# Moving GpSimd's steps of a woven-in chain two gathers later, and one accumulation three rows later

## The reference

```python
u_sel = jnp.take(u, idx, axis=0)
act = jax.nn.gelu(jnp.einsum("chkd,cd->chk", u_sel, xc))
v_sel = jnp.take(v, idx, axis=0)
return jnp.einsum("chk,chkd->cd", act * gates, v_sel)
```

## Time and profile before

| what | value |
| --- | --- |
| median of 3 runs | 2394.14 us (2394.11 to 2395.13) |
| the profiled execution's own time | 2392.49 us |
| its span | 2390.5 us |
| TensorE, VectorE, ScalarE, GpSimd busy | 85%, 74%, 49%, 30% of the span |
| mean rate of the transfers | 325 GB/s over the span |

### The profile page before, as it was taken

How to read it: one execution, slowest core, us unless ns; L and a number is a source line. 1 busy time by engine, 2 the same in 40 slices (tenths; PEclk the granted TensorE clock), 3 DMA queues, 4 the chain that set the end, 5 groups by cost and what they waited for, 6 DMA issues and landing times. The chain is left out here.

```text
span 2390.5 us, 29684 instructions
## 1 busy us (share of the span) xinstructions
PE 2041.0 (85%) x9896; PEld 1414.8 (59%) x9896; DVE 1768.2 (74%) x3454; ACT 1174.1 (49%) x3850; POOL 728.1 (30%) x637
## 2 busy tenths in 40 slices
PE   8899897687875568999666687799989999999999
PEld 8544442243331127874343565588459978898997
DVE  6589876766778878889899988766765646756564
ACT  4355566665565563433455554433344435444443
POOL 0134434453444443233365633433310001100000
PEclk9999998998986688999885798899989999999999
DMA  9199999999999998999999999999976544224553
GB/s 361 72 398 421 415 384 351 398 395 404 398 415 387 395 396 344 400 421 420 362 405 356 376 421 420 399 417 421 421 295 208 177 166 146 89 89 159 194 178 139
DMA packets 109767, 777.72 MB, mean 325 GB/s; under 512 B 12320, under 2 KB 13088, under 8 KB 16688
## 3 DMA queue, kind: packets, MB, share of 16 engines
q0 software_dynamic: 73728, 536.90, 55.6%
q1 hardware_dynamic: 35888, 238.93, 26.0%
HBM read 773.69 MB, written 2.10 MB: 325 GB/s over the span
## 5 line engine op out<-in xcount | busy, mean ns | idle before, releaser
L2102 ACT ACTIVATE smalls<-smalls 128x1 f32<-128x1 f32 (+1 forms) x2058 | 541.3, 287 | 716.8 <-DVE smalls L2006 698.9
L2830 POOL DMA_INDIRECT pair<-in_uv,idx x512 | 609.5, 1190 | 913.5 <-DVE resid L1265 495.8
L663 PE MATMUL bank<-pair,diag 128*64 128x512 f32 (+1 forms) x1056 | 314.2, 710 | 142.5 <-ACT diag L2102 142.2
L2006 DVE CUSTOM_DVE_ANT_0 pair<-pair,hd 128x1024 f32<-128x1024 f32 x256 | 311.7, 1221 | 148.2 <-DMA pair<-in_uv,idx 147.2
L663 PE MATMUL bank<-ft,raw 128*128 128x256 f32 x1664 | 371.1, 385 | 17.9 <-DVE ft L1259 17.9
L663 PEld LDWEIGHTS bank<-ft,raw 128*128 128x128 f32 x1664 | 321.3, 194 | 63.4 <-issue 18.4
L2006 DVE CUSTOM_DVE_ANT_0 pair<-pair,hn 128x1024 f32<-128x1024 f32 x256 | 312.2, 1220 | 56.9 <-DMA pair<-in_uv,idx 56.4
L1265 DVE SCALAR_TENSOR_TENSOR resid<-pair,smalls,resid 128x1024 f32<-128x1024 f32 x243 | 310.8, 1279 | 0.7 <-ACT smalls L2102 0.6
L1259 DVE TENSOR_TENSOR half<-raw,half 128x1024 fp32r<-128x1024 f32 (+2 forms) x184 | 212.0, 1191 | 122.7 <-ACT half L2102 121.2
L663 PEld LDWEIGHTS bank<-pair,diag 128*64 128x64 f32 (+1 forms) x1056 | 77.2, 155 | 319.3 <-ACT diag L2102 191.4
L2102 ACT ACTIVATE half<-raw 128x1024 fp32r<-128x1024 f32 (+2 forms) x184 | 179.5, 1023 | 90.9 <-PE bank L663 90.8
(11 more groups left out here) (328 smaller groups left out, 3183.1 us busy)
## 6 DMA issues: line engine op xcount, KB each, us to landing
raw<-in_wts SPq DMA_DIRECT2D x199, 1024.0 KB, 8.9
pair<-in_wts SPq DMA_DIRECT2D x11, 1024.0 KB, 16.8
pair<-in_uv,idx POOLq DMA_INDIRECT x512, 10.7
raw<-in_wts SPq DMA_DIRECT2D x10, 512.0 KB, 6.2
raw<-in_wts SPq DMA_DIRECT2D x4, 720.0 KB, 6.1
resid<-in_x SPq DMA_DIRECT2D x4, 512.0 KB, 12.0
out<-resid SPq DMA_DIRECT2D x8, 256.0 KB, 5.7
raw<-in_wts SPq DMA_DIRECT2D x2, 768.0 KB, 6.5
```

The lines of the kernel that those rows point to most:

```text
L663: return e.matmul(o, a, b, start=start, stop=stop)
L2006: e.tensor_tensor_reduce(b[:, 0:1024], b[:, 0:1024], x_, 1.0, 0.0, ALU.mult, ALU.add, actv[:, i % 8:i % 8 + 1]).then_inc(dotted, 1)
L2102: return e.activation(o, i, f, **kw)
L2830: e.indirect_dma_start(pair[i % NPAIR], None, uv, bass.IndirectOffsetOnAxis(ap=idx[:, n % SLOTS, k:k + 1], axis=0)).then_inc(pairs_in[i % ...
```

## The change

Two numbers are changed. GpSimd does the steps of chain A two gathers later in its order: a step that stood ahead of gather i stands ahead of gather i + 2. And VectorE adds the banks of the third tile (`mixed_in(2, ...)`) in its row 271 instead of 268. No instruction is added or taken away.

```diff
                     for strand in strands:
                         strand.until(i)
-                    if i == HALF + 12:
+                    if i == HALF + 15:
                         mixed_in(2, i - 1)
                         for h in range(2):
                             taken(e, "mix", 4 + h)
...
             first, between = Paced(chain("A")), Paced(rest())
             for i in range(PAIRS):
                 n, k = divmod(i, 16)
-                first.until(clock(i - 8))
+                first.until(clock(i - 10))
                 between.until(i)
```

## The result

The changed kernel takes 2405.14 us (median of 7 runs, 2399.74 to 2410.42), the kernel before 2393.32 us (7 runs, 2386.42 to 2395.13). The ratio is 1.0061, 95% interval 1.0046 to 1.0075: 14.6 us more, between 11 and 18 (the two medians lie 11.8 us apart). The prediction was 2408.0 us, range 2397 to 2414, "slower" at 0.81. Its forecast case came true. Run again later, beside the kernel before on the same chip, the changed kernel gave 1.0058 (1.0037 to 1.0080).

The account below looks back on a forecast made before the run. TensorE and the DMA transfers were taken to be at their limit together. Terms -1.3 + 0 + 2.8 + 6.7 + 1.0 + 4.7 sum to +13.9 us, giving a median of 2408 us, range 2397 to 2414.

Parts of the forecast that it names:

- forecast case: Whole kernel: the likeliest outcome, +10 to +19 us, 2404 to 2413 us, chance 0.55.
- mixed_in: Moved from row 268 to 271, it lets TensorE's first up-projection start earlier: -1.3 us, bounds 0 and -1.3.
- first norm's rates: Run after gather 271 instead of before 270; VectorE has no wait: 0 us, upper bound +1.
- second norm: Rates behind gather 336 make VectorE and the latent projection wait: +2.8 us, bounds 0 and +3.8.
- latent and head rates: VectorE 9.5 us late at row 351, less 2.8 of gather waits: +6.7 us, bounds +3 and +9.5.
- attention's head rates: Pairs used at rows 366 and 384; gather waits cover VectorE's delay, gathers land later: +1 us, bounds -2 and +5.
- third norm: Rates behind gather 448 make VectorE wait, and all reaches the end: +4.7 us, bounds +2.3 and +5.3.
- row rule: GpSimd steps due at row d run once VectorE added row d+4, not d+2; uses four rows after due stall.
- its own 5 us are covered there: Attention, 1378 to 1450 us: VectorE's 13.4 us of gather waits cover its own 5 us delay.
- Rival 1: Norms and head rates: the queue of transfers hides much of the stalls, +5.4 us, 2399.5 us, chance 0.22.
- Rival 2: GpSimd's steps: none of their move reaches the end, only mixed_in is left, 2393 us; chance 0.11 including mixtures.
- Rival 3: Transfer holes, above all at 1270 us, go as gathers aren't held behind steps: faster, 2385 us, chance 0.07.

Follow-up runs that it names:

- again: The changed kernel's second run and profile, both edits unchanged, against the kernel before on the same chip: 2405.66 against 2391.08 us, ratio 1.0058.
- i - 6: All of GpSimd's steps two gathers earlier than in the kernel before, mixed_in left in row 268: ratio 0.9971 (0.9960 to 0.9982).
- i - 7: All of GpSimd's steps one gather earlier than in the kernel before, mixed_in left in row 268: ratio 0.9992 (0.9979 to 1.0004).
- mixed_in alone: Only mixed_in moved to row 271, GpSimd's order that of the kernel before: ratio 0.9998 (0.9983 to 1.0014).
- i - 9: All of GpSimd's steps one gather later than in the kernel before, mixed_in left in row 268: ratio 1.0015 (1.0003 to 1.0027).
- latent and head rates alone: Only the three latent rates and four head rates of fq and fk two gathers later than in the kernel before: ratio 1.0031 (1.0017 to 1.0045).

## Why the prediction was right, term by term

| term | predicted | measured by rows |
| --- | --- | --- |
| mixed_in | -1.3 (0 to -1.3) | -0.5, -1.3 again, -1.6 alone, at row 273 |
| first norm's rates | 0 | 0, no wait at L1259 |
| second norm | +2.8 (0 to 3.8) | +2.9 in four profiles |
| latent and head rates | +6.7 (3 to 9.5) | +7.8 - 1.6 = +6.2 |
| attention's head rates | +1.0 (-2 to +5) | +6.1 - 2.7 = +3.4 |
| third norm | +4.7 (2.3 to 5.3) | +5.1 to +6.2 |
| sum | +13.9 | +17.6 by rows 267 to 511; +14.6 by the runs' ratio |

The total came out nearer than its terms, and that is in part luck. By rows the loss is 3.7 us more than forecast: attention was 2.4 us dearer, mixed_in gave 0.8 less, and 0.9 lie in rows 333 to 343, for which there was no term. That the runs gave 14.6 and not 17.6 no term accounts for either.

**The row rule** carried the forecast. Every use that it named as late is late, and the first norm, used five rows after its steps are due, is not. But two uses that also come five rows after are late in attention: at row 371 VectorE waits 1.24 us, which the prediction didn't have, and at row 384 it waits 1.43 and 0.85 (its "other pair"). There the last gather's issue and a head rate take some 3.7 us together (1336.17 to 1339.8 us at row 384, 1294.24 to 1298.05 at row 371), and a row of VectorE's only 2.4, so one row of room is not enough. The waits at ft of 2.78 and 5.01 us were forecast as 2.8 and 4.7. For GpSimd VectorE waits 18.2 us where some 15 were forecast. In the term of the latent and head rates two misses cancel: VectorE is 7.8 us late at row 351 and not 9.5, but gets only 1.6 us back from the waits for gathers and not 2.8.

**Attention was the mis-sized term**, the step "its own 5 us are covered there". The 13.4 us of waits for gathers of the earlier trace rows did not swallow the delay: waits shrank by 2.8 to 4.1 us, and 3.4 us reached row 443 in the changed kernel, 3.8 in the experiment with this part alone. That VectorE waits for transfers later on does not make a delay ahead of it free: while it stands no buffer comes free and no gather leaves. The windows below, under the rivals, show that.

**mixed_in** was right at its place and its start (1.35 us), but how much of it shows at row 273 differs with the granted clock. A loss of cover at row 271 did not occur: the wait for fsg is still 2.33 us.

**The rivals.** Rival 1, transfers that hide much, needed the gathers' waits to shrink by some 15 of the 21.3 us of new ones; they shrank by 5.4. Rival 2 fell at the first look at the waits. Rival 3 named a hole in the transfers at 1270 us, DMA share 0.51. It did close there, and opened again behind VectorE's stall of 3.78 us. In the changed kernel (the DMA share is the last but one column):

```profile
1270.00:1275.00 5.00, 1.51 (x6) 1.19 (x6) 5.00 (x8) 3.04 (x16) 3.92 (x4) 0.50 0.92 346
1275.00:1280.00 5.00, 1.54 (x6) 1.19 (x6) 2.14 (x4) 3.28 (x16) 4.50 (x4) 0.50 0.88 316
1280.00:1285.00 5.00, 2.06 (x11) 2.00 (x11) 3.16 (x6) 0.00 (x0) 2.43 (x2) 0.50 0.86 336
1285.00:1290.00 5.00, 1.06 (x5) 0.70 (x5) 5.00 (x8) 2.92 (x13) 2.38 (x2) 0.50 0.13 28
```

By 1285 next to nothing was left under way, and the next gather was issued only at 1287.03, after GpSimd had waited 4.61 us for VectorE's row. Over 1262 to 1300 us the share is 0.84 in both kernels, and 0.82 from 1270 to 1308, where the changed kernel does about the rows that the kernel before does from 1262 to 1300: the hole was moved, not filled. What the rival needed, steps done before their uses, is what `i - 6` has.

**The Trainium skill**, "SBUF — State Buffer", section "Summary: rules for kernel authors", has it that a GpSimd operation that reads SBUF and a VectorE operation with two inputs in SBUF block each other for whole instructions. The trace agrees in direction: the three latent rates take 2.06 us while VectorE stands waiting, 3.26 in the earlier trace rows; a pair of head rates takes 3.30 us in a wait and 5.26 with `i - 7` while VectorE works. By the prediction's estimate from that rule the term would have been 1.7 us lower. That is by how much the delay at row 351 stayed below the 9.5 us forecast, 1.2 of it the latent rates'; the term itself ended only 0.5 lower, as less came back from the waits for gathers. No run sets this lock apart from other causes.

## What to carry to other kernels

Where one in-order engine issues transfers and small steps of a chain, count for each step the rows between the row that its place in the queue waits for and the row that uses it: places with no row of room each cost a transfer's issue and the step. At the two norms the cost reached the last row in full, at the latent and head rates in part. Places with one row of room cost too where the issue and the step take longer than a row. Try the other direction too: one gather earlier cost nothing here, two gained 7 us by the medians. A later wait for transfers covers a delay only in part when the buffers come free by the delayed engine's own rows.

## What the runs showed of the hardware beyond that

- At the first up-projection, after 6 to 13 us in which TensorE stood idle, its granted clock rose from 0.50 to 1.00 (1.2 to 2.4 GHz) at 3.5 us (mixed_in alone), 4.0 (before), 4.1 (after, again), 4.5 (`i - 6`) or 5.6 us (after) behind the start of the same matmuls. Over all fourteen profiles it is 3.3 to 6.0 us, and both ends are kernels with mixed_in at row 268 (`i - 9`; latent and head rates alone). Each us of it costs 0.5 us at row 273: with that taken off, the eight profiles with mixed_in at row 268 agree with the kernel before to 0.02 us, and the six with row 271 are 1.2 to 1.4 us earlier. Before it is taken off, the eight average +0.1 us and the six -0.8 us. So the small gain at row 273 in the changed kernel is mixed_in's whole gain beside a late rise; whether the earlier start itself puts the rise off is not shown.
- Executions differ before any edit acts: row 250 starts between 839.0 and 849.6 us in fourteen profiles, and in the two of the changed kernel at 843.9 and 839.0. Only differences between rows of one execution could tell the terms apart.
